# A mixture-of-experts stage whose gathered and scattered rows move as 1 KB quarters, with VectorE turning them and the down weights stationary

## The chip, the cores and the metric

The kernel runs on one core of one Trainium2 chip. The metric is the device time of one launch in microseconds (us). Only the last stage of the kernel, the mixture of experts, is touched by the change, along with the few instructions that lead into it.

## The reference

One layer of a hybrid decoder: an input projection, a depthwise convolution branch and an RWKV-7 recurrence branch, an output projection and a LayerNorm give `x` for 520 tokens (512 prompt tokens and 8 sample tokens) of width 1024, all in float32. Then the part that matters here:

```
scores = sigmoid(x @ router_w)                 # 64 experts, top 8 per token by groups
gates  = chosen scores / their sum * 2.5
for each expert e, for the tokens t that chose it:
    h = silu(x[t] @ exp_gate[e]) * (x[t] @ exp_up[e])        # 1024 -> 256
    f[t] += gates[t, e] * (h @ exp_down[e])                  # 256 -> 1024
f += shared expert;   y = LayerNorm(ALPHA * x + f)
```

There are 520 x 8 = 4160 pairs of token and expert, 65 per expert in the mean.

## The kernel before

**Stages.** Up to some 475 us the core projects, convolves, runs the recurrence, mixes, routes and computes the shared expert. `x` is written to DRAM as `scr_x1`, the residual with the shared expert as `scr_f`. Then the expert stage runs 64 jobs, one per expert, each with up to `CAP` = 96 tokens (an overflow path for experts with more tokens follows it; its loops are skipped at run time when there are none). The last stage reads `scr_f` back, normalises it and stores the result.

**One job q.** Its steps, each in a function of its own:

- `build_member` (VectorE) compares each token's position in the expert's list with 0 to 95 and so makes a 0/1 matrix of tokens by slots. `make_list` (TensorE) multiplies it with a table, so that each of the 96 slots gets its token's tile, row and weight (the weight in three bfloat16 parts). `read_list` (VectorE) turns that into a row number (slots without a token get a number past the end, which the DMA skips) and a weight.
- `gather` (GpSimd) fetches the 96 rows of `scr_x1`, 4 KB each, with one indirect DMA, into `x_list`: slots on partitions, 1024 columns along. `turn_list` (TensorE, eight transposes into PSUM) and `copy_turned` (ScalarE, two copies) make `x_list_t`: columns on partitions, slots along.
- `gate_up` (TensorE): weights stationary, in halves of 64 columns that land on partitions 0 to 63 and 64 to 127, the 96 slots moving; 128 instructions. `gate_act` (ScalarE sigmoid) and `gate_mul` (VectorE, two products) make `hid`.
- `down` (TensorE): `hid` stationary, 96 columns, the down weights moving, 512 at a time, 8 instructions. The result has slots on partitions. `weigh_act` (ScalarE) and `weigh_dve` (VectorE) multiply one half each by the gates on the way out of PSUM, into `y_list`, which has two buffers.
- `add_rows` (GpSimd) adds the 96 rows to `scr_f` with one accumulating indirect DMA. It waits for the scatter of the job before, as two experts may add to one row of `scr_f`, and an accumulating DMA reads before it writes.

**What sets the order.** Each engine has one queue with the jobs written out in order. For TensorE, at each q: the list of job q+4, gate_up of q+1, the turn of q+2, down of q. For GpSimd: the gather of q+4, then the scatter of q. For VectorE: read_list of q+4, gate_mul of q+1, build_member of q+5, weigh_dve of q. SyncE loads the weights, 1 MB each for gate, up and down, into six slots: gate and up of job q+6 are issued when gate_up(q) is done, down of q+5 when down(q-1) is done. `gathered`, `added` and the others are semaphores; a DMA raises its own by 16 when it has landed.

**Lines in the profile.** L2303 is the matmul of gate_up, L2331 that of down, L2278 the transposes, L869 make_list, L882 to L890 read_list, L858 build_member, L2312 gate_act, L2319 and L2321 gate_mul, L2288 copy_turned, L2341 and L2349 the two weighs, L900 the gather, L2358 the scatter, L913, L919 and L925 the loads of gate, up and down.

## Time and profile before

| | |
|---|---|
| time, median of 3 runs | 1145.57 us (1140.51 to 1149.66) |
| profiled execution, its span | 1144.7 us (its time outside the span is not shown) |
| TensorE busy | 1076.1 us, 94% |
| VectorE, ScalarE, GpSimd busy | 540.9, 280.5, 180.2 us |
| moved by the DMA engines | 278.79 MB |
| packets of GpSimd's DMA queue (q0) | 14336, 34.11 MB |

The span runs from the first to the last instruction. GpSimd's busy time is that of issuing its DMAs, not of their transfers. "Landing" in the DMA views is the time from an issue until its semaphore has risen.

### The profile page before, as it was taken

What the parts mean: (1) busy time and instruction counts of PE and PEld (TensorE: products, weight loads), DVE (VectorE), ACT (ScalarE), POOL (GpSimd) and SP (SyncE); (2) the same over time, 40 slices, a digit from 0 to 9 for tenths busy, and PEclk for the clock granted to TensorE, in tenths of its full rate; (3) what the DMA queues carried; (4) which work ended last, traced back from release to release, by engine and by line L of the source; (5) the groups of instructions that cost most, each with busy time, mean ns of one, the idle gap of its engine ahead of it and who ended that gap; (6) DMA issues with size and microseconds to landing.
All of it is one profiled execution on the core that took longest, in us unless ns stands there. A gap on an engine that the chain in (4) does not pass through costs nothing.

```text
span 1144.7 us, 33418 instructions
## 1 busy us (share of the span) xinstructions
PE 1076.1 (94%) x14942; PEld 814.8 (71%) x14943; DVE 540.9 (47%) x1208; ACT 280.5 (25%) x596; POOL 180.2 (16%) x198
## 2 busy tenths in 40 slices
PE   7999998887899999999999999999999999999990
PEld 6877886765653567677777777777777777777760
DVE  0789969698665778553222222222222222222215
ACT  2156411122337111111111111111111111111114
POOL 2000100000000002122222222122222222222210
PEclk9999999989669999999999999999999999999995
DMA  7222131220425557799999999999999999999734
GB/s 215 74 56 56 50 82 41 49 74 5 162 74 203 172 191 299 282 351 372 368 355 357 362 363 362 359 361 359 366 361 368 364 362 360 363 363 352 221 48 160
DMA packets 87365, 278.79 MB, mean 244 GB/s; under 512 B 22331, under 2 KB 46916, under 8 KB 62381
## 3 DMA queue, kind: packets, MB, share of 16 engines
q1 hardware_dynamic: 71941, 239.29, 57.1%
q0 software_dynamic: 14336, 34.11, 12.6%
q10 hardware_dynamic: 944, 3.24, 0.8%
q8 instruction: 119, 1.95, 0.7%
q14 instruction: 25, 0.20, 0.1%
HBM read 258.80 MB, written 34.52 MB: 256 GB/s over the span
## 4 chain that ended last, share of the span: by engine, by line
PE 67%; DVE 9%; issue 2%; ACT 2%; DMA 1%; SPq 0%; POOLq 0%; DVEq 0%; ACTq 0%
PE ph L2303 30%; PE ph L2331 19%; PE pst L2278 4%; PE ph L1496 2%; PE pz_late L2278 2%; DVE w_exp L163 2%; PE pt L869 1%; PE pst L1392 1%; PE pt L1411 1%; PE ph L1621 1%; PE ph L1478 1%; PE pz_late L1436 1%; PE pz_late L1437 1%; PE pt L1405 1%; PE pt L1414 0%
## 5 line engine op out<-in xcount | busy, mean ns | idle before, releaser
L2303 PE MATMUL ph<-arena,w_exp 128*64 128x96 f32 x8192 | 352.5, 247 | 0.0
L2303 PEld LDWEIGHTS ph<-arena,w_exp 128*64 128x64 f32 x8192 | 340.4, 138 | 4.2 <-issue 3.1
L2331 PE MATMUL ph<-w_exp,arena 128*96 128x512 f32 x512 | 230.5, 593 | 1.2 <-DVE arena L2321 1.2
L2358 POOL DMA_INDIRECT scr_f<-arena,row x64 | 92.3, 1443 | 472.0 <-DMA scr_f<-arena,row 230.1
L2319 DVE TENSOR_TENSOR arena<-arena,ph 128x192 f32<-128x192 f32 x64 | 22.7, 355 | 287.8 <-ACT arena L2312 287.8
L507 PE MATMUL pz<-w_exp 128*128 128x260 f32 x672 | 158.4, 394 | 0.3 <-ACT w_exp L322 0.3
L2331 PEld LDWEIGHTS ph<-w_exp,arena 128*96 128x96 f32 x512 | 80.2, 167 | 103.8 <-issue 102.3
L507 PEld LDWEIGHTS pz<-w_exp 128*128 128x128 f32 x672 | 129.3, 195 | 23.3 <-issue 2.9
L2349 DVE TENSOR_SCALAR arena<-ph,weight 96x512 f32<-96x512 f32 x64 | 47.8, 746 | 174.2 <-PE ph L2331 174.1
L2312 ACT ACTIVATE arena<-ph 128x192 f32<-128x192 f32 x64 | 21.1, 330 | 416.0 <-PE ph L2303 416.0
L163 DVE SCALAR_TENSOR_TENSOR w_exp<-arena,w_exp 128x512 f32<-128x512 f32 x120 | 90.0, 750 | 3.8
L900 POOL DMA_INDIRECT x_area<-scr_x,row x64 | 62.8, 982 | 39.4 <-issue 33.9
L2341 ACT ACTIVATE arena<-ph,weight 96x512 f32<-96x512 f32 x64 | 43.6, 682 | 86.1 <-PE ph L2331 76.6
L1496 PE MATMUL ph<-w_exp 128*128 128x512 f32 x128 | 57.9, 605 | 0.0
L2278 PE MATMUL pst<-ident,x_area 96*128 96x96 f32 x320 | 50.8, 289 | 0.0
L869 PEld LDWEIGHTS pt<-table,member 128*96 128x96 bf16 x320 | 24.3, 124 | 36.1 <-issue 35.7
L2278 PEld LDWEIGHTS pst<-ident,x_area 96*128 96x128 f32 x320 | 40.3, 202 | 7.6 <-issue 0.4
L2288 ACT COPY arena<-pst 128x480 f32<-128x480 f32 x64 | 35.7, 558 | 39.5 <-PE pst L2278 39.5
L1496 PEld LDWEIGHTS ph<-w_exp 128*128 128x128 f32 x128 | 24.3, 195 | 29.6 <-issue 29.0
L858 DVE TENSOR_TENSOR member<-slot_index,position 128x480 bf16<-128x480 f32 x64 | 41.6, 651 | 0.0
L2278 PE MATMUL pz_late<-ident,x_area 96*128 96x96 f32 x192 | 31.8, 275 | 0.0
L1478 PE MATMUL ph<-x_area,w_exp 128*128 128x260 f32 x128 | 29.1, 385 | 0.7 <-ACT arena L1826 0.7
(359 smaller groups left out, 1076.4 us busy)
## 6 DMA issues: line engine op xcount, KB each, us to landing
w_exp<-in_exp_up_dram SPq DMA_DIRECT2D x64, 1024.0 KB, 17.3
w_exp<-in_exp_down_dram SPq DMA_DIRECT2D x64, 1024.0 KB, 16.5
w_exp<-in_exp_gate_dram SPq DMA_DIRECT2D x64, 1024.0 KB, 13.7
w_exp<-in_w_in_dram SPq DMA_DIRECT2D x22, 512.0 KB, 3.9
w_exp<-in_x_prompt_dram SPq DMA_DIRECT2D x8, 512.0 KB, 5.2
w_exp<-in_w_out_dram SPq DMA_DIRECT2D x2, 2048.0 KB, 11.5
scr_x<-arena SPq DMA_DIRECT2D x4, 512.0 KB
scr_f<-arena ACTq DMA_DIRECT2D x4, 512.0 KB, 3.6
```

What stands on the lines that cost most here:

```text
L163: self.ch.link(self.nc.vector.scalar_tensor_tensor(out, u, w, out, ALU.mult, ALU.add))
L507: last = nc.tensor.matmul(banks(pz[0:w, c % 2, :])[:, b, :], m.w_col[:, c % WB, k, 0:w], halves(m.x_t[:, k, :])[:, b, :], start=(k == 0), ...
L858: nc.vector.tensor_tensor(m.member[:, s % 2], m.slot_index[:].unsqueeze(1).broadcast_to([P, NT, CAP]), src.unsqueeze(2).broadcast_to([P, N ...
L900: nc.gpsimd.indirect_dma_start(m.x_list[:, s, :], None, m.scr_x1, bass.IndirectOffsetOnAxis(ap=m.row[:, job.l:job.l + 1], axis=0), bounds_ ...
L1478: last = nc.tensor.matmul(banks(ph[:, 1 - part, :])[:, b, :], sh_w[part][:, k, j * P:(j + 1) * P], halves(x1_t[:, k, :])[:, b, :], start=( ...
L1496: last = nc.tensor.matmul(ph[0:n, i % 2, c * 512:(c + 1) * 512], lhs, w_out[c][:, kw, :], start=(part == 0 and k == 0), stop=(part == 1 an ...
L2278: last = nc.tensor.transpose(px[bank][:, at * CAP:(at + 1) * CAP], v[:, k, :], m.ident[0:CAP, 0:CAP])
L2303: last = nc.tensor.matmul(pgu[64 * half:64 * half + 64, s % 2, (2 * part + j) * CAP:(2 * part + j + 1) * CAP], w[job.slot][:, k, f0:P * ha ...
L2331: last = nc.tensor.matmul(pyl[0:CAP, c, :], hid[:, s % 2, j, :], m.expert_down[job.slot][:, j, c * 512:(c + 1) * 512], start=(j == 0), sto ...
L2341: nc.scalar.activation(y_list[:, s % 2, 0:512], pyl[0:CAP, 0, :], ACT.Copy, scale=weight[:, job.l:job.l + 1]).then_inc(y_act, 1)
L2349: nc.vector.tensor_scalar(y_list[:, s % 2, 512:1024], pyl[0:CAP, 1, :], weight[:, job.l:job.l + 1], None, ALU.mult).then_inc(y_dve, 1)
L2358: nc.gpsimd.indirect_dma_start(m.scr_f, bass.IndirectOffsetOnAxis(ap=row[:, job.l:job.l + 1], axis=0), y_list[:, s % 2, :], None, bounds_c ...
```

## The change

- `x_list` becomes `x_pieces`: each gathered row of 4 KB is fetched as four quarters of 1 KB (`QUADS`, `QW` = 256). Partition 32 * quad + t of run r holds quarter `quad` of slot 32 * r + t, so one indirect DMA fetches 32 slots, 128 pieces, and a job has three (`RUNS`). The scatter does the same with three DMAs that all raise `added`; `add_rows` of the next job waits for all three.
- VectorE turns 32 x 32 blocks (`turn_pieces`) straight into `x_list_t`; the eight transposes and the two copies go.
- `down` holds the down weights stationary in 64-column halves and moves `hid` (96 columns): 64 instructions of gate_up's form, in two PSUM areas by turns (the banks of the old transposes serve as the second). The result has columns on partitions; `turn_y` (VectorE, two turns) turns it back into `y_pieces`, and `weigh` (ScalarE, three activations in place) multiplies by the gates.
- `make_list` holds the table stationary and moves the member matrix, so that the list comes out along the free dimension; `read_list` turns it with one 32 x 96 VectorE transpose and writes row numbers and weights four times, one for each quarter.
- The order on VectorE becomes: read_list of q+4, turn_pieces of q+2, build_member of q+5, gate_mul of q+1, turn_y of q. The counting of overflow jobs moves into the stage; some small tiles move into other memory.

The core of the diff:

```
+QUADS = 4
+QW = D // QUADS
+RUNS = CAP // 32
 def make_list(...):
-        last = nc.tensor.matmul(pl[0:CAP, s % 2, 0:6], m.member[:, s % 2, i, :],
-                                m.table[:, bass.ds(q, 1), i, :].rearrange("p o c -> p (o c)"),
+        at = (q * NT + i) * 6
+        last = nc.tensor.matmul(pl[0:32, s % 2, 0:CAP], m.table_rows[:, at:at + 32], m.member[:, s % 2, i, :],
                                 start=(i == 0), stop=(i == NT - 1))
 def read_list(...):
-    nc.vector.tensor_copy(entry[:, s, :], pl[0:CAP, s % 2, 0:6]).then_inc(m.entry_ready, 1)
+    nc.vector.transpose(entry[:].rearrange("t r j -> t (r j)"), pl[0:32, job.s % 2, 0:CAP]).then_inc(m.entry_ready, 1)
     dve.wait_ge(m.entry_ready, q + 1)
-    (tensor_scalar, scalar_tensor_tensor, tensor_tensor, tensor_reduce of 96 x 1)
+    ch.link(nc.vector.scalar_tensor_tensor(found[:, :, 0], entry[:, :, 0], float(P), entry[:, :, 1], ALU.mult, ALU.add))
+    ch.link(nc.vector.scalar_tensor_tensor(found[:, :, 0], entry[:, :, 2], -float(TT), found[:, :, 0], ALU.mult, ALU.add))
+    for quad in range(QUADS):
+        last = nc.vector.tensor_scalar(m.piece_row[32 * quad:32 * (quad + 1), s, :], found[:, :, 0],
+                                       float(QUADS), float(QUADS * TT + quad), ALU.mult, ALU.add)
+    last.then_inc(m.pieces_ready, 1)
+    ch.link(nc.vector.tensor_reduce(found[:, :, 1], entry[:, :, 3:6], AX, ALU.add))
+    for quad in range(QUADS):
+        last = nc.vector.tensor_copy(m.piece_weight[32 * quad:32 * (quad + 1), s, :], found[:, :, 1])
+    last.then_inc(m.weight_ready, 1)
 def gather(...):
-    nc.gpsimd.indirect_dma_start(m.x_list[:, s, :], None, m.scr_x1, ...).then_inc(m.gathered[s], 16)
+    for r in range(RUNS):
+        nc.gpsimd.indirect_dma_start(m.x_pieces[:, s, r, :], None, m.scr_x1.rearrange("t (q c) -> (t q) c", q=QUADS),
+                                     bass.IndirectOffsetOnAxis(ap=m.piece_row[:, job.l, r:r + 1], axis=0),
+                                     bounds_check=QUADS * TT - 1, oob_is_err=False).then_inc(m.gathered[s], 16)
-    def turn_list(pe, job): ...      def copy_turned(act, job): ...
+    def turn_pieces(dve, job):
+        q, s = job.q, job.s
+        dve.wait_ge(gathered[s], 16 * RUNS * (job.turn + 1))
+        if job.has_before(2):
+            dve.wait_ge(gu_done, q - 1)
+        nc.vector.transpose(x_list_t[:, s % 2].rearrange("p k (r t) -> p r k t", r=RUNS),
+                            m.x_pieces[:, s].rearrange("p r (c k) -> p r k c", k=KD)).then_inc(x_ready, 1)
 def down(pe, job):
+        if job.has_before(2):
+            pe.wait_ge(y_turned, 2 * (q - 1))
+        for k in range(KD):
+            bank, at = (0, k) if k < KA else (1, k - KA)
             for j in range(2):
-                last = nc.tensor.matmul(pyl[0:CAP, c, :], hid[:, s % 2, j, :], m.expert_down[job.slot][:, j, c * 512:(c + 1) * 512], ...)
+                for half in range(2):
+                    d0 = 512 * half + k
+                    last = nc.tensor.matmul(py_t[s % 2][bank][64 * half:64 * half + 64, at * CAP:(at + 1) * CAP],
+                                            m.expert_down[job.slot][:, j, d0:512 * half + 512:KD], hid[:, s % 2, j, :], ...)
-    def weigh_act(act, job): ...     def weigh_dve(dve, job): ...
+    def turn_y(dve, job):
+        for bank, (k0, k1) in enumerate(((0, KA), (KA, KD))):
+            dve.wait_ge(y_done, 2 * q + bank + 1)
+            if job.has_before(2) and bank == 0:
+                dve.wait_ge(added[s % 2], 16 * RUNS * job.pair)
+            nc.vector.transpose(y_pieces[:, s % 2].rearrange("p r (c k) -> p r k c", k=KD)[:, :, k0:k1, :],
+                                py_t[s % 2][bank][:, 0:(k1 - k0) * CAP].rearrange("p (k r t) -> p r k t", r=RUNS, t=32)).then_inc(y_turned, 1)
+    def weigh(act, job):
+        act.wait_ge(y_turned, 2 * q + 2)
+        act.wait_ge(weight_ready, q + 1)
+        for r in range(RUNS):
+            last = nc.scalar.activation(y_pieces[:, s % 2, r, :], y_pieces[:, s % 2, r, :], ACT.Copy,
+                                        scale=piece_weight[:, job.l, r:r + 1])
+        last.then_inc(y_weighed, 1)
 def add_rows(pool, job):
-        pool.wait_ge(y_act, q + 1)
-        pool.wait_ge(y_dve, q + 1)
+        pool.wait_ge(y_weighed, q + 1)
         if job.has_before(1):
-            pool.wait_ge(added[(s + 1) % 2], 16 * job.before)
+            pool.wait_ge(added[(s + 1) % 2], 16 * RUNS * job.before)
-        nc.gpsimd.indirect_dma_start(m.scr_f, ..., y_list[:, s % 2, :], ..., compute_op=ALU.add).then_inc(added[s % 2], 16)
+        for r in range(RUNS):
+            nc.gpsimd.indirect_dma_start(m.scr_f.rearrange("t (q c) -> (t q) c", q=QUADS),
+                                         bass.IndirectOffsetOnAxis(ap=piece_row[:, job.l, r:r + 1], axis=0), y_pieces[:, s % 2, r, :], None,
+                                         bounds_check=QUADS * TT - 1, oob_is_err=False, compute_op=ALU.add).then_inc(added[s % 2], 16)
```

## Rows read from the trace of the kernel before

**Rows 1.** The page: busy time and share of each engine, and DMA in 40 slices.

```profile
PE 1076.1 (94%) x14942; PEld 814.8 (71%) x14943; DVE 540.9 (47%) x1208; ACT 280.5 (25%) x596; POOL 180.2 (16%) x198
DMA  7222131220425557799999999999999999999734
```

**Rows 2.** Chain of waits, 700 to 712 us: start, length, what.

```profile
699.92 5.43 PE ph L2303 x128
705.36 0.72 PE pst L2278 x5
706.08 0.33 PE pz_late L2278 x3
706.42 3.44 PE ph L2331 x8
709.85 0.18 PE pt L869 x5
710.04 1.96 PE ph L2303 x43
```

**Rows 3.** Timeline of GpSimd, 700 to 760 us: start, length, what, idle before.

```profile
702.45 1.44 POOL L2358 DMA_INDIRECT scr_f<-arena,row  x1 [6.70 <-DMA scr_f<-arena,row]
704.19 0.98 POOL L900 DMA_INDIRECT x_area<-scr_x,row  x1 [0.30 <-issue]
713.12 1.44 POOL L2358 DMA_INDIRECT scr_f<-arena,row  x1 [7.95 <-DMA scr_f<-arena,row]
```

**Rows 4.** The scatter: landings in 490-560 us, 640-1040 us (with GpSimd's wait), 1118-1121 us.

```profile
DMA to landing us min/median/max: 6.8/7.7/9.0
...
  DMA scr_f<-arena,row: 227.0, 30
...
DMA to landing us min/median/max: 7.9/9.3/10.4
...
DMA to landing us min/median/max: 4.9/4.9/4.9
```

**Rows 5.** DMA queues, 700 to 760 us: packets, MB, share of 16 engines.

```profile
q1 hardware_dynamic: 2534, 18.45, 80.9%
q0 software_dynamic: 1309, 3.04, 20.6%
```

**Rows 6.** DMA queue 1, 20 to 60 us, packets of 512 bytes.

```profile
q1 hardware_dynamic: 5258, 2.65, 24.4%
```

**Rows 7.** Timeline of SyncE's queue, and the last down load's landing (1060 to 1072 us).

```profile
477.21 0.33 SPq L913 DMA_DIRECT2D w_exp<-in_exp_gate_dram  x1
...
1063.85 0.33 SPq L925 DMA_DIRECT2D w_exp<-in_exp_down_dram  x1
...
DMA to landing us min/median/max: 15.0/15.0/15.0
```

**Rows 8.** Timeline: first scatter, last weigh, last scatter, first load of the last stage.

```profile
489.28 1.50 POOL L2358 DMA_INDIRECT scr_f<-arena,row  x1 [8.37 <-DVE row L889]
...
1118.02 0.75 DVE L2349 TENSOR_SCALAR arena<-ph,weight 96x512 f32<-96x512 f32 x1 [3.77 <-PE ph L2331]
...
1119.61 1.40 POOL L2358 DMA_INDIRECT scr_f<-arena,row  x1 [6.27 <-DVE arena L2349]
1124.64 2.15 SPq L2389 DMA_DIRECT2D w_exp<-scr_f  x5
```

**Rows 9.** Stretches of 10 us: busy PE, PEld, DVE, ACT, POOL, clock, DMA share, GB/s.

```profile
240.00:250.00 10.00, 8.23 (x175) 6.04 (x172) 9.55 (x15) 2.69 (x4) 0.00 (x0) 0.68 0.05 13
700.00:710.00 10.00, 10.00 (x151) 7.70 (x149) 2.54 (x10) 1.87 (x4) 2.41 (x2) 1.00 1.03 360
```

**Rows 10.** Groups of instructions, 700 to 760 us: busy us, mean ns | idle before.

```profile
L2349 DVE TENSOR_SCALAR arena<-ph,weight 96x512 f32<-96x512 f32 x6 | 4.5, 746 | 16.9 <-PE ph L2331 16.9
L2341 ACT ACTIVATE arena<-ph,weight 96x512 f32<-96x512 f32 x6 | 4.1, 682 | 7.2 <-PE ph L2331 7.2
...
L885 DVE TENSOR_SCALAR spare<-entry,minus_spare,spare_row 96x1 f32<-96x1 f32 x6 | 1.6, 269 | 0.2
L889 DVE TENSOR_TENSOR row<-spare,token 96x1 uint32<-96x1 f32 x6 | 0.9, 155 | 0.2
```

More of the change, by code:

```diff
@@ L833, in lists @@
     m.x_area = sb("x_area", [P, KD * TT])
-    m.x_list = m.x_area[0:CAP, 0:NB * D].rearrange("t (s d) -> t s d", s=NB)
+    m.x_pieces = view(m.x_area, 0, NB, RUNS, QW)
+    m.AT_BEHIND = NB * RUNS * QW
+    m.job_expert = view(m.x_area, m.AT_BEHIND, m.EXTRA)
     m.member = sb("member", [P, 2, NT, CAP], BF16)
-    m.entry = sb("entry", [CAP, STEPS, 6])
-    m.row = sb("row", [CAP, STEPS], U32)
-    m.spare = sb("spare", [CAP, STEPS])
-    m.token = sb("token", [CAP, STEPS])
-    m.weight = sb("weight", [CAP, STEPS])
+    m.entry = sb("entry", [32, RUNS, 32])
+    m.found = sb("found", [32, RUNS, 2])
+    m.piece_row = sb("piece_row", [P, STEPS, RUNS], U32)
+    m.piece_weight = sb("piece_weight", [P, STEPS, RUNS])
     m.member_ready = sem("member_ready")
@@ L877, in read_list @@
     q, s = job.q, job.l
-    entry, spare, token, row, weight = m.entry, m.spare, m.token, m.row, m.weight
+    entry, found = m.entry, m.found
     dve.wait_ge(m.list_done, q + 1)
     if job.has_before(STEPS):
-        dve.wait_ge(m.added[s % 2], 16 * (job.pair - STEPS // 2 + 1))
-    nc.vector.tensor_copy(entry[:, s, :], pl[0:CAP, s % 2, 0:6]).then_inc(m.entry_ready, 1)
+        dve.wait_ge(m.added[s % 2], 16 * RUNS * (job.pair - STEPS // 2 + 1))
+    nc.vector.transpose(entry[:].rearrange("t r j -> t (r j)"), pl[0:32, job.s % 2, 0:CAP]).then_inc(m.entry_ready, 1)
@@ L1835, in store_f @@
                     act.dma_start(m.scr_f[t0:t0 + n, :], x1[0:n, i, :]).then_inc(m.f_stored[i], 16)
-                for i in range(TM - 1):
+                for i in range(TM):
                     store_f(i)
-                work.copy_turned(act, Job(0))
-                store_f(TM - 1)
                 act.wait_ge(f_done, NT)
@@ L1844, in _ @@
                 last.then_inc(sample_moved, 1)
-                work.copy_turned(act, Job(1))
                 store_f(TM)
@@ L2165, in experts @@
     hid = view(m.arena, m.AT_INVERSE + 4 * CAP, 2, 2, CAP)
-    y_list = view(m.arena, m.AT_X1, 2, D)[0:CAP]
+    y_pieces = view(m.arena, m.AT_X1, 2, RUNS, QW)
     jobs3 = view(m.arena, m.AT_X1 + 2 * D, m.EXTRA, E)
@@ L2185, in experts @@
     o_gate, o_up, o_down = m.expert_gate[0], m.expert_up[0], m.expert_down[0]
-    o_place = sb("o_place", [P, NT])
-    o_entry = sb("o_entry", [CAP, 6])
+    o_at = m.AT_BEHIND + m.EXTRA
+    o_place = view(m.x_area, o_at, NT)
+    o_entry = view(m.x_area, o_at + 8, 6)[0:CAP]
     o_row = sb("o_row", [CAP, 1], U32)
-    o_spare = sb("o_spare", [CAP, 1])
-    o_token = sb("o_token", [CAP, 1])
-    o_weight = sb("o_weight", [CAP, 1])
-    o_x_list = x_list[:, 0, :]
+    o_spare, o_token, o_weight = (view(m.x_area, o_at + 16 + i, 1)[0:CAP] for i in range(3))
+    assert o_at + 19 <= KD * TT
+    o_x_list = m.x_area[0:CAP, 0:D]
     o_x_list_t = x_list_t[:, 0]
@@ L2195, in experts @@
     o_hid = hid[:, 0]
-    o_y_list = y_list[:, 0, :]
+    o_y_list = view(m.arena, m.AT_X1, D)[0:CAP]
     o_member = m.member[:, 0]
@@ L2326, in down @@
         pe.wait_ge(m.down_loaded[job.slot], job.filled)
-        for c in range(2):
-            if job.has_before(1):
-                pe.wait_ge((y_act, y_dve)[c], q)
+        if job.has_before(2):
+            pe.wait_ge(y_turned, 2 * (q - 1))
+        for k in range(KD):
+            bank, at = (0, k) if k < KA else (1, k - KA)
             for j in range(2):
-                last = nc.tensor.matmul(pyl[0:CAP, c, :], hid[:, s % 2, j, :], m.expert_down[job.slot][:, j, c * 512:(c + 1) * 512],
-                                        start=(j == 0), stop=(j == 1))
-            last.then_inc(y_done, 1)
@@ L2475, in vector @@
                 count_jobs(q)
-            weigh_dve(dve, Job(q))
+            turn_y(dve, Job(q))
             if q + 2 == E:
@@ L2535, in scalar @@
                 gate_act(act, Job(q + 1))
[L2536 to L2537 removed]
+            weigh(act, Job(q))
             if q + 2 == E:
@@ L2705, in kernel_program @@
         m.cnt = sb("cnt", [P, 4, E])
-        m.table = sb("table", [P, E, NT, 6], BF16)
+        m.table_rows = sb("table", [P, E * NT * 6 + 32], BF16)
+        m.table = view(m.table_rows, 0, E, NT, 6)
         m.w_exp = sb("w_exp", [P, SLOTS * EXPERT_FLOATS])
```

112 lines of the change are left out of this document (37 added, 75 removed).

## Prediction

> **What bounds the kernel now.** I read the views from coarse to fine. The page's busy line and slices come first [rows 1]: TensorE is busy 94% of the span, GpSimd 16%, and from the middle of the span on the DMA row stands at 9 in every slice. In a 10 us window of the stage TensorE is busy all 10.00 us at full clock and the DMA share is 1.03 [rows 9]. So in the expert stage TensorE and the DMA engines are both full, and it must be settled which of them a shorter TensorE job would leave as the limit. The reader should see there that "TensorE 94%" is not yet an answer.
>
> The chain of waits gives TensorE's job [rows 2]. From one gate_up to the next (699.92 to 710.04) is 10.12 us: 5.43 for 128 gate and up matmuls, 1.05 for eight transposes (0.72 and 0.33), 3.44 for the eight down matmuls, 0.18 for the list. Nothing waits in between. Sixty-four such jobs are the stage.
>
> GpSimd's timeline [rows 3] shows the second chain, which the share of 16% hides. add_rows(q) may be issued only when the scatter of q-1 has landed, so scatters are serial: issued at 702.45 for 1.44 us, the next at 713.12, a period of 10.67. The tile view has the landing [rows 4], and it counts from the start of the issue: the last scatter starts at 1119.61, lands 4.9 later, and the loads of f that wait for it start at 1124.64 [rows 8]. Taken from the end of the issue, a landing is 7.7 - 1.4 = 6.3 us early in the stage (median), 9.3 - 1.4 = 7.9 in the middle and 3.5 for the very last, which has the DMA engines to itself. Between a release and the issue GpSimd loses another 0.9: weigh_dve ends at 1118.02 + 0.75 = 1118.77, the scatter starts at 1119.61 [rows 8]. So the middle stands at 1.4 + 7.9 + 0.9 = 10.2 us per job and more in single ones. In that stretch GpSimd waited for a scatter 30 times, 227.0 us [rows 4]. This chain is already as long as TensorE's job; the spare buffer of y_list lets it lag a little.
>
> The DMA view gives the third [rows 5]. In 60 us, 5.93 jobs of 10.12, the weight queue took 80.9% and GpSimd's queue 20.6% of 16 engines: together 1.015 x 60 / 5.93 = 10.3 us of DMA per job. The loads tell the same another way [rows 7]: job 6's gate is issued at 477.21, the last down weights at 1063.85, and they land 15.0 later, at 1078.9: 602 us for 58 jobs, 10.38 each. They never had slack to go faster. Three resources thus sit between 10.1 and 10.7 us per job, and the change shortens one of them.
>
> **The change part by part.** TensorE: the eight transposes go (-1.05). The down product becomes 64 instructions (8 k x 2 j x 2 halves, two instructions each as in gate_up) of the very form of gate_up, 64 columns stationary, 96 moving: 64 x 5.43/128 = 2.71, against 3.44 (-0.73). The list's five matmuls move 96 columns in place of 6: bounded by 0.18 as now and by 5 x 0.042 x 2 = 0.42; I take 0.3. TensorE's job is 5.43 + 2.71 + 0.3 = 8.4 us, 1.7 less. If TensorE alone were the limit, that would be 64 x 1.7 = 109 us. It is not.
>
> VectorE: in a 10 us window it is busy 2.54 [rows 9]. Out go weigh_dve (0.75) and the old read_list (five instructions, 0.15 to 0.27, about 0.87) [rows 10]. In come the new read_list, twelve instructions of 0.15 to 0.27 (1.8 to 3.2), and two turns of 768 elements per partition each, for which no row exists: at the 746 ns of 512 elements [rows 10] each is 1.1, and twice that is my upper end for the strided read and write. Sum: 0.92 + 1.8..3.2 + 2.2..4.4 = 4.9 to 8.5 us. I take 6.3. That fits beside the other work, and nothing behind it on the engine is late: gate_mul(q+1) is needed only after gate_up(q+2). If the turns cost three times my row, it would stand at 10 and join the others.
>
> ScalarE: the two copies and one weigh go, three weighs of 256 elements come, each at most the 0.68 of the 512-element one [rows 10]: with what stays, at most some 2.4 us of a job, free either way. Dropping the job counting ahead of the first residual gives VectorE about 3 us back and the longer read_lists take about that; I count 0. The arena moves, table padding and the overflow path cost nothing here: no overflow job runs in the trace.
>
> GpSimd: each gather and each scatter becomes three indirect DMAs of 128 rows of 1 KB in place of one of 96 rows of 4 KB. The issue of 96 rows takes 1.44 (scatter) and 0.98 (gather) [rows 3]. For 128 rows the cost lies between the same and 128/96 of it: 1.44 to 1.92, and 0.98 to 1.31. With 0.3 between neighbours (704.19 against the end of the scatter before it), a job's scatters take 4.9 to 6.4 us to issue and the gathers 3.8 to 4.8. I take 5.6 and 4.3, since a list of row addresses is written out entry by entry and half of the step is the middle. GpSimd would be busy near 9 us of a job, not 2.4.
>
> DMA work: the bytes stay. The descriptors do not: now 1309 packets of GpSimd's queue in 5.93 jobs are about 221, by the layout 192 rows and 32 completions. After, 6 x 128 rows and 96 completions make 864, 640 more. What one more costs beside its bytes is at least nothing, and at most what a whole 512-byte packet takes, 24.4% x 16 x 40 us / 5258 = 29.7 ns [rows 6]: 640 / 16 x 0.0297 = 1.2 us per job. I take 0.6, so 10.9 us of DMA per job.
>
> The serial scatter chain is then what ends last. Its period is the issue of all three pieces, the landing of the third from the end of its issue, and GpSimd's 0.9: add_rows waits for all 48 completions of a job, not 16. The landing is bounded by 3.5, the quiet end, and 7.9, the loaded middle [rows 4, 8]. The last piece carries a third of the bytes, but its two forerunners are queued before it and the weight queue shares the engines. With the period above the DMA work per job, the weight queue is empty part of the time, which is nearer to the early stretch (6.3) and the quiet end than to the middle: I take 5.6. Period 5.6 + 5.6 + 0.9 = 12.1 us; ends 4.9 + 3.5 + 0.9 = 9.3 (then another resource decides) and 6.4 + 7.9 + 0.9 = 15.2. The gathers' 4.3 us of issue hide inside the 5.6 of landing. What waits behind: turn_y(q) on VectorE waits for the scatter of q-2, and down(q+2) for turn_y(q), so the whole stage falls into step, TensorE idling 4 us of each job.
>
> The sum, on the profiled execution (span 1144.7, 0.9 below the median of the three runs; the rest of the difference I leave out). First scatter at 489.3 [rows 8]; 63 periods of 12.1 = 762.3; the last issue 5.6 and a quiet landing 3.5; and from there to the end of the span what it takes now, 1144.7 - (1119.6 + 4.9) = 20.2. Together 1280.9, say 1280 us, +135.
>
> One rule of the Trainium skill speaks the other way on the landing. By the page "DMA: Bandwidth & Descriptors", section "Anatomy of one DMA", a GpSimd-issued DMA takes about 2.0 us plus its bytes at 436 GB/s: an estimate of 2.3 us for one 128 KB piece, and a period of 8.8, which would be no limit at all. For the present 384 KB it gives 2.9; the quiet landing of 3.5 comes near that, the loaded 7.9 is nearly three times as long, so the trace agrees only where nothing else moves, and I keep the rows. The same page, "Rules for kernel authors", asks to coalesce small transfers into large ones; the change does the reverse.
>
> **The rivals.** (a) The pieces land quickly, the chain hides, and DMA work decides. The condition is a chain under about 10.9, which the low ends allow (9.3). The loads would then end at 1078.9 + 58 x (0 to 1.2), and after them come the last down (2.7), turn (1.1), weigh (1.3), GpSimd's 0.9, issue (5.6), landing (3.5) and the 20.2: 1078.9 + 35.3 = 1114.2, up to 1184; with 0.6 it is 1149. For it: the last piece is small, and the load queue is deep now only because it is saturated. Against: a saturated queue is just what lengthens landings, 6.3 to 7.9 in the same kernel.
>
> (b) The faster side of that, under 1134: it holds only if a quarter row costs nearly nothing beside its bytes (less than 0.34 us a job) and the chain stays under 10.4. Then the gain is at most 31 us, since the loads can't end before 1079: TensorE's 109 us can't be had in any case. I see no row for both conditions at once.
>
> (c) The small pieces get one turn each beside 8 KB weight packets. A job has 48 such turns per engine and the weight queue only 24 packets, so pieces lag, landing grows past 7.9 and the period is 14.5 to 16: 489.3 + 63 x 15 + 29.3 = 1464. In its favour, the 7.9 of now is already long for six rows per engine. A second mechanism leads to the same place: with TensorE idle a third of the time its granted clock may fall to half, as it did in a window ahead of the stage, 0.68 with 8.23 us busy of 10 [rows 9]; 8.4 us of work at a mean of 0.6 is 14.
>
> (d) VectorE's turns cost three times my row and more (over 3.3 us each) and VectorE at 11 us or above becomes the limit: like the forecast in time, and told from it by a VectorE that is busy over 90%.
>
> **How the numbers follow.** A chain period of 11.1 to 13.9 (1218 to 1394), the forecast, with (d) in it: 0.62. (a) without its fast part, 1134 to 1184, and the stretch up to 1218: 0.18. (b): 0.08. (c): 0.12. The range leaves out (b), the part of (a) under 1145, and most of (c): 1145 to 1405. A measurement of this kernel can tell about 1% from no change, 11.5 us either way (its three runs span 0.8%): faster by more than that needs under 1134, 0.09; within it 1134 to 1157, 0.07; slower 0.84.
>
> **What would show it.** Right, if GpSimd's share rises from 16% to over 60%, its queue shows near 55,300 packets (864 x 64, from 14,336), three scatter issues of 1.4 to 1.9 us stand together, the next three some 12 us later, VectorE's turn_y waits for the scatter, TensorE's job shows 5.43 + 2.71 with a gap of about 4 us, and the DMA row falls below 9. Wrong in the landing if the period is about 11 with the DMA row at 9; wrong in the issue if the pieces take under 1 us or over 2; wrong altogether if TensorE stays without gaps at 8.4.

## Result, and the profile after

The changed kernel takes 1323.6 us (median of four runs, 1317.3 to 1326.0); the kernel before takes 1147.2 in the same comparison. The ratio is 1.153, with a 95% interval of 1.148 to 1.158. The forecast was 1280 us.

The page of the changed kernel, beside [rows 1] and [rows 5]: busy time by engine, clock and DMA by slice, and the two queues.

```profile
PE 1106.5 (84%) x18014; PEld 981.0 (75%) x18015; DVE 789.6 (60%) x1784; ACT 260.3 (20%) x596; POOL 531.2 (40%) x455
...
PEclk9989998887999989899889889889889889889985
DMA  6211222104646679889888898879789879888534
...
q1 hardware_dynamic: 71941, 239.29, 50.3%
q0 software_dynamic: 36864, 34.20, 13.8%
```

No engine is full any more. TensorE fell from 94 to 84% of the span, the DMA row is no longer all nines, and the clock row alternates 9 and 8. GpSimd's queue went from 14,336 to 36,864 packets.

One stretch of 300 us in the expert stage, before and then after (columns as in [rows 9]):

```profile
700.00:1000.00 300.00, 300.00 (x4459) 232.83 (x4458) 78.96 (x270) 55.21 (x119) 70.54 (x58) 1.00 1.02 363
```

```profile
700.00:1000.00 300.00, 249.22 (x4533) 243.17 (x4531) 150.65 (x414) 35.79 (x92) 181.19 (x138) 0.89 0.87 288
```

TensorE was busy without a gap at full clock; now it is busy 249 us at a mean granted clock of 0.89. The DMA share fell to 0.87, so the weight queue is no longer kept full.

The period comes from the first scatter issue of the first and of the last job. The timeline of the changed kernel, GpSimd and the first load of the last stage:

```profile
491.66 1.64 POOL L2353 DMA_INDIRECT scr_f<-arena,piece_row  x1 [9.86 <-ACT arena L2342]
...
1286.18 1.55 POOL L2353 DMA_INDIRECT scr_f<-arena,piece_row  x1 [2.75 <-issue]
...
1289.91 1.56 POOL L2353 DMA_INDIRECT scr_f<-arena,piece_row  x1 [0.30 <-issue]
1293.80 2.15 SPq L2385 DMA_DIRECT2D w_exp<-scr_f  x5
```

(1286.18 - 491.66) / 63 = 12.61 us per job. In the kernel before it was (1119.61 - 489.28) / 63 = 10.01 [rows 8]. 63 x 2.60 = 164 us of the 170.5 by which the span grew (1144.7 to 1315.2). "Period" below is always this quotient; it is a mean over the whole stage, and the jobs of the stretch from 700 to 1000 us are a little longer (23 of them here, 13.0 us each).

The same timeline from 804 us on shows what ends a period:

```profile
804.45 1.07 DVE L2334 STREAM_TRANSPOSE arena<-pst 128x480 f32<-128x480 f32 x1 [5.79 <-DMA scr_f<-arena,piece_row]
...
805.21 1.63 POOL L2353 DMA_INDIRECT scr_f<-arena,piece_row  x1 [3.30 <-issue]
...
807.14 1.57 POOL L2353 DMA_INDIRECT scr_f<-arena,piece_row  x1 [0.30 <-issue]
...
809.02 1.58 POOL L2353 DMA_INDIRECT scr_f<-arena,piece_row  x1 [0.30 <-issue]
...
810.84 0.39 PE L874 MATMUL pt<-member,table 128*32 128x96 bf16 x5 [2.00 <-DVE member L862]
...
818.23 1.59 DVE L2334 STREAM_TRANSPOSE arena<-ph 128x480 f32<-128x480 f32 x2 [6.80 <-DMA scr_f<-arena,piece_row]
...
818.99 1.62 POOL L2353 DMA_INDIRECT scr_f<-arena,piece_row  x1 [4.34 <-issue]
```

Three issues end at 810.60. The DMA lands, VectorE's turn_y starts at once (818.23, 7.6 later), and the next job's first issue follows 0.76 behind it. "issue" in GpSimd's row is its own latency after a wait that just ended; the release is seen on the VectorE row. TensorE's idle time has moved to the list: VectorE stands in turn_y's wait, so build_member behind it is late and the list waits for it. The waits of 700 to 1000 us sum this up (us, times, longest):

```profile
DVE arena L2334 <- DMA scr_f<-arena,piece_row: 142.1, 23, 9.2
...
PE pt L874 <- DVE member L862: 50.2, 16, 5.4
```

TensorE's work in one early job, at full clock (timeline):

```profile
484.31 0.39 PE L874 MATMUL pt<-member,table 128*32 128x96 bf16 x5
484.63 5.51 PE L2291 MATMUL ph<-arena,w_exp 128*64 128x96 f32 x128
489.96 2.60 PE L2322 MATMUL pst<-arena,w_exp 128*64 128x96 f32 x40
492.40 1.64 PE L2322 MATMUL pz_late<-arena,w_exp 128*64 128x96 f32 x24
493.97 0.39 PE L874 MATMUL pt<-member,table 128*32 128x96 bf16 x5
```

From start to start: 0.32 for the list, 5.33 for gate_up, 4.01 for down, 9.66 together. Groups of the stretch from 700 on, to be read beside [rows 2] and [rows 10]:

```profile
L2291 PE MATMUL ph<-arena,w_exp 128*64 128x96 f32 x2946 | 151.1, 272 | 0.2 <-issue 0.2
L2322 PE MATMUL ph<-arena,w_exp 128*64 128x96 f32 x768 | 49.3, 285 | 0.3 <-issue 0.3
...
L2276 DVE STREAM_TRANSPOSE arena<-x_area 128x768 f32<-128x768 f32 x23 | 36.2, 1572 | 0.8 <-DMA x_area<-scr_x,piece_row 0.2
```

gate_up's mean is 272 ns, against 247 in the kernels whose stretch has full clock. That is the lower clock: the list and gate_up that follow a wait of 3.46 us, from 824.50 on, run with the clock halved (the row below, 0.50), while the gate_up from 811.15 on, at 1.00, takes 5.50 us as a whole. The turn of x stands at 1.57 us.

```profile
824.00:829.00 5.00, 4.50 (x55) 4.36 (x57) 1.06 (x3) 0.00 (x0) 3.48 (x4) 0.50 0.92 270
```

### The profile page after: what moved, and what is told of

Same layout as the page of the kernel before. It is cut to its first block and busy times, and to the rows that moved or that the text cites. A ratio compares the mean times of both kernels' runs of the same rounds, so it can differ in the third digit from the quotient of the medians.

```text
span 1315.2 us, 40523 instructions
## 1 busy us (share of the span) xinstructions
PE 1106.5 (84%) x18014; PEld 981.0 (75%) x18015; DVE 789.6 (60%) x1784; ACT 260.3 (20%) x596; POOL 531.2 (40%) x455
## 3 DMA queue, kind: packets, MB, share of 16 engines
q0 software_dynamic: 36864, 34.20, 13.8%
## 5 line engine op out<-in xcount | busy, mean ns | idle before, releaser
L2291 PE MATMUL ph<-arena,w_exp 128*64 128x96 f32 x8192 | 409.6, 268 | 6.4 <-issue 6.4
L2353 POOL DMA_INDIRECT scr_f<-arena,piece_row x192 | 306.0, 1594 | 265.6 <-issue 247.1
L2291 PEld LDWEIGHTS ph<-arena,w_exp 128*64 128x64 f32 x8192 | 397.5, 155 | 13.1 <-issue 7.2
L908 POOL DMA_INDIRECT x_area<-scr_x,piece_row x192 | 200.1, 1042 | 73.0 <-issue 72.7
L2342 ACT ACTIVATE arena<-arena,piece_weight 128x256 f32<-128x256 f32 x192 | 83.7, 498 | 682.0 <-DVE arena L2334 682.0
L2334 DVE STREAM_TRANSPOSE arena<-pst 128x480 f32<-128x480 f32 x32 | 34.2, 1069 | 196.7 <-DMA scr_f<-arena,piece_row 187.7
L2322 PE MATMUL ph<-arena,w_exp 128*64 128x96 f32 x2048 | 131.3, 285 | 0.4 <-issue 0.3
L2322 PEld LDWEIGHTS ph<-arena,w_exp 128*64 128x64 f32 x2048 | 128.3, 219 | 0.6 <-issue 0.5
L2276 DVE STREAM_TRANSPOSE arena<-x_area 128x768 f32<-128x768 f32 x64 | 101.0, 1577 | 9.1 <-DMA x_area<-scr_x,piece_row 7.3
L2322 PE MATMUL pst<-arena,w_exp 128*64 128x96 f32 x1280 | 84.6, 288 | 4.5 <-DVE arena L2309 4.4
L2322 PEld LDWEIGHTS pst<-arena,w_exp 128*64 128x64 f32 x1280 | 81.5, 219 | 4.9 <-DVE arena L2309 4.6
L896 DVE COPY piece_weight<-found 32x3 f32<-32x3 f32 x256 | 56.9, 222 | 4.9
L2322 PE MATMUL pz_late<-arena,w_exp 128*64 128x96 f32 x768 | 53.0, 288 | 0.0
```

What stands on the lines that cost most here:

```text
L896: last = nc.vector.tensor_copy(m.piece_weight[32 * quad:32 * (quad + 1), s, :], found[:, :, 1])
L908: nc.gpsimd.indirect_dma_start(m.x_pieces[:, s, r, :], None, m.scr_x1.rearrange("t (q c) -> (t q) c", q=QUADS), bass.IndirectOffsetOnAxis( ...
L2276: nc.vector.transpose(x_list_t[:, s % 2].rearrange("p k (r t) -> p r k t", r=RUNS), m.x_pieces[:, s].rearrange("p r (c k) -> p r k c", k=K ...
L2291: last = nc.tensor.matmul(pgu[64 * half:64 * half + 64, s % 2, (2 * part + j) * CAP:(2 * part + j + 1) * CAP], w[job.slot][:, k, f0:P * ha ...
L2322: last = nc.tensor.matmul(py_t[s % 2][bank][64 * half:64 * half + 64, at * CAP:(at + 1) * CAP], m.expert_down[job.slot][:, j, d0:512 * hal ...
L2334: nc.vector.transpose(y_pieces[:, s % 2].rearrange("p r (c k) -> p r k c", k=KD)[:, :, k0:k1, :], py_t[s % 2][bank][:, 0:(k1 - k0) * CAP]. ...
```

## Experiments

Times are medians; the ratio with its interval is to the kernel before in the same comparison. Each kernel's row of 700 to 1000 us has the columns shown above.

**1. two_targets.** Even and odd jobs add into two tensors, so a scatter never waits for the one ahead of it. The odd experts' part is left out of the result.

```
-        if job.has_before(1):
-            pool.wait_ge(added[(s + 1) % 2], 16 * RUNS * job.before)
-            nc.gpsimd.indirect_dma_start(m.scr_f.rearrange(...
+            nc.gpsimd.indirect_dma_start((m.scr_f, m.scr_g)[s % 2].rearrange(...
```

> The changed kernel, with even experts added into scr_f and odd ones into a second tensor, both filled with the same residual; the last stage reads only the first, so the odd experts' part is left out of y. add_rows no longer waits for the scatter of the job before, only (through turn_y) for the one two jobs back. Serial scatter chain (my theory): the period of 12.6 us falls to the next limit, GpSimd's own six issues (about 9.7 us), TensorE's 9.65 us or the DMA work (10.4 to 10.9): 10.5 us, time near 1190. Rival, TensorE with its throttled clock is the limit: TensorE's job is untouched, time stays above 1290. Rival, DMA work is already the limit: also above 1290.

Measured: 1268.1 us, ratio 1.108 (1.104 to 1.112), period 11.69. The window:

```profile
700.00:1000.00 300.00, 272.61 (x4979) 252.47 (x4976) 169.10 (x465) 42.30 (x103) 199.02 (x151) 0.98 0.94 309
```

TensorE's timeline of the same kernel (start, length, what, idle before):

```profile
804.90 2.11 PE L2292 MATMUL ph<-arena,w_exp 128*64 128x96 f32 x45
807.27 0.33 PE L2292 MATMUL ph<-arena,w_exp 128*64 128x96 f32 x2 [0.26 <-issue]
808.02 0.39 PE L2292 MATMUL ph<-arena,w_exp 128*64 128x96 f32 x4 [0.43 <-issue]
808.76 0.41 PE L2292 MATMUL ph<-arena,w_exp 128*64 128x96 f32 x4 [0.35 <-issue]
```

The chain was a limit: without it 55 us go, and no wait for a scatter is left. But the time stays 78 us above what I expected, and neither rival (above 1290) holds. The new thing is in the rows: in the middle of gate_up TensorE pauses, about every 0.74 us, for 0.2 to 0.45 us, and the profile names nothing that it waits for. None of my cases had this.

**2. few_weight_bytes.** From the seventh job on only an eighth of each expert's weights is loaded (the rest of a slot keeps older weights); the chain stays.

```
+    n = KD * FE if q < SLOTS else KD * FE // 8
-    ...gate[s].rearrange("p k f -> p (k f)"), one_expert(m.exp_gate, q))
+    ...gate[s].rearrange("p k f -> p (k f)")[:, 0:n], one_expert(m.exp_gate, q)[:, 0:n])
```

> The changed kernel, with only an eighth of each expert's weights loaded from job 6 on (the rest of a slot keeps old weights, so y is another). Same instructions and waits, 7 MB in place of 58 x 3 MB. If the landing of a scatter is long because the weight packets share the engines, it falls from 7.6 to about 3.5 us after the last issue, the period to 5.4 + 3.5 + 0.8 = 9.7 us, and the time to about 1140. If a landing is long by itself (small descriptors, read and write of scr_f), the period stays near 12.6 and the time at 1310 to 1325.

Measured: 1268.6 us, ratio 1.109 (1.104 to 1.114), period 11.69.

```profile
700.00:1000.00 300.00, 273.00 (x4964) 253.85 (x4966) 167.18 (x451) 40.95 (x100) 199.49 (x151) 0.98 0.41 77
```

Its gate_up in the same stretch, from the groups:

```profile
L2294 PE MATMUL ph<-arena,w_exp 128*64 128x96 f32 x3239 | 165.6, 253 | 24.8 <-issue 24.5
```

The time is neither of the two that I expected (an eighth of 58 x 3 MB is 22 MB, not the 7 written there, which changes nothing in the argument). With the DMA engines at 0.41 the landings are short enough that the chain drops out. GpSimd's timeline:

```profile
813.48 1.55 POOL L2356 DMA_INDIRECT scr_f<-arena,piece_row  x1 [0.30 <-issue]
...
819.38 1.63 POOL L2356 DMA_INDIRECT scr_f<-arena,piece_row  x1 [0.30 <-issue]
```

The third piece is issued until 815.03, and the next job's first piece starts at 819.38, right behind three gathers, without having waited, so the landing took under 4.4 us. The same stretch, from the end of the last issue to the release, is 7.6 in the timeline above. So much of a landing is contention with the weight queue. The rest is the same as in experiment 1 to 1 us: the same period and the same pauses (24.5 against 24.4 us of the stretch). The second limit is not DMA load.

**3. down_contiguous.** The 64 stationary columns of down lie side by side, not 8 apart; y has its columns permuted.

```
-                    d0 = 512 * half + k
-                   m.expert_down[job.slot][:, j, d0:512 * half + 512:KD], ...
+                    d0 = 512 * half + 64 * k
+                   m.expert_down[job.slot][:, j, d0:d0 + 64], ...
```

> The changed kernel, with down's stationary operand read as 64 neighbouring columns instead of every eighth (the columns of y come out in another order). The profile shows down at 4.0 us where 2.7 was counted; if the stride is what makes it dear, down shows about 2.7 us here. Serial scatter chain: TensorE is not what ends last, so the time moves by less than 1% (1310 to 1330), unless the longer idle time lowers its clock further. Rival, TensorE is the limit: 64 x 1.3 = 83 us less, near 1240.

Measured: 1321.5 us, ratio 1.156 (1.150 to 1.161): no change from the changed kernel, as the chain theory has it. The groups of its TensorE:

```profile
L2322 PE MATMUL ph<-arena,w_exp 128*64 128x96 f32 x768 | 34.2, 246 | 0.4 <-issue 0.4
...
L2322 PEld LDWEIGHTS ph<-arena,w_exp 128*64 128x64 f32 x768 | 32.8, 137 | 0.6 <-issue 0.6
```

Those 768 matmuls took 49.3 us in the changed kernel and take 34.2 here; a weight load falls from 219 to 137 ns. gate_up, whose columns lie 2 apart, has 138 ns in the kernel before, whose whole stage runs at full clock. So a stride of 8 floats costs, and one of 2 doesn't.

**4 and 5. before_two_issues, before_four_issues.** The kernel before, with only its scatter cut into two issues of 512 columns or four of 256.

```
+        for r in range(n):
+            c = slice(1024 // n * r, 1024 // n * (r + 1))
+            ...indirect_dma_start(m.scr_f.rearrange("t (q c) -> (t q) c", q=n), ...part_row[:, job.l, r:r + 1]...,
+                                  y_list[:, s % 2, c], None, ...
```

> The kernel before, whole in every part but the scatter, which goes out as two indirect DMAs of 96 half rows of 2 KB (VectorE makes the two index columns). Serial scatter chain: issue 2 x 1.44 + 0.3 = 3.2 us, landing 6.3 to 7.9, 0.9 for GpSimd: period 10.4 to 12.0, time 1170 to 1270, near 1215. Rival, the cost of the change lies in the small descriptors, the turns or TensorE: at most 0.3 us of DMA work more per job, time 1145 to 1165.

> The kernel before, whole, with each job's scatter in four indirect DMAs of 96 quarter rows of 1 KB: as many descriptors as the changed kernel's scatter, one issue more. Theory: issue 4 x 1.41 + 0.9 = 6.5 us, landing after the last at least 4 and at most 7.5, GpSimd 0.8: period 11.3 to 14.8, time 1225 to 1440, near 1280. Two issues gave 10.35 per job; if a landing shrinks by as much as the issue grows, as it nearly did there, the period is 10.7 to 11 and the time 1185 to 1205.

Measured: 1166.2 us, ratio 1.019 (1.015 to 1.024), period 10.35, and 1298.4 us, ratio 1.133 (1.129 to 1.137), period 12.48. The four-issue kernel's window:

```profile
700.00:1000.00 300.00, 264.83 (x3582) 194.89 (x3581) 72.50 (x337) 43.65 (x96) 164.73 (x122) 0.93 0.92 296
```

Its longest waits:

```profile
ACT arena L2348 <- DMA scr_f<-arena,part_row: 174.3, 24, 12.0
DVE arena L2356 <- DMA scr_f<-arena,part_row: 164.5, 20, 11.3
```

And its gate_up:

```profile
L2310 PE MATMUL ph<-arena,w_exp 128*64 128x96 f32 x3072 | 132.1, 247 | 0.0
```

This is the chain theory by itself: one issue, two, four give 10.0, 10.35, 12.5 us per job. With one or two there is still slack (TensorE busy 298.4 of 300 with two), with four the chain is the limit. Two issues came out just below the range that I expected (1170 to 1270), since the slack swallowed most; four came out inside theirs. From two issues to four a job's issuing grows from 3.14 to 6.58 us, but what lies between its end and the next job's first issue shrinks from 7.27 to 5.80 (medians over the GpSimd timelines), so two more issues lengthen the period by 2.1 us, not by 3.4. Part of the 7.27 was slack, and early pieces can land while later ones are issued; how much is which is not shown. And a split scatter puts no pauses into gate_up (0.0).

**6 and 7. quarter_gather_only, quarter_gather_two_targets.** The changed kernel's gather in three pieces and VectorE's turn of x, with the down product, the weighing and the one whole-row scatter of before; in the second, two targets as well (odd experts left out).

```
-        for r in range(RUNS):
-            ...indirect_dma_start(m.scr_f.rearrange(...), ...piece_row[:, job.l, r:r + 1]..., y_pieces[:, s % 2, r, :], ...
+        ...indirect_dma_start(m.scr_f, ...row[:, job.l:job.l + 1]..., y_list[:, s % 2, :], ...
```

> The changed kernel with its second half undone: gather in 1 KB quarters and the VectorE turn stay, down, the two weighs and the scatter (one DMA of 96 rows of 4 KB) are those of the kernel before; both lists are made, which adds five small matmuls and five small VectorE instructions. Theory (the cost is the serial chain of a job's scatters): the chain is again 1.44 + 7.9 + 0.9 = 10.2 us, TensorE's job 9.4, DMA work 10.4: time 1140 to 1165. Rival (the small gather pieces lie in the queue ahead of the scatters and lengthen landings): period near 10.9, time near 1195. Rival (TensorE throttled or starved): above 1200.

> The kernel of quarter_gather_only, with odd experts added into a second tensor and no wait on the scatter before; the second tensor is left out of y. TensorE's job is 9.4 us, GpSimd about 6, the scatter chain spans two jobs. Theory: DMA work (10.4 us a job, loads end at 1079 or later) is what is left: 1110 to 1135, faster than before. Rival: the landings never mattered with whole rows, TensorE's 9.4 with gaps in its instruction supply leaves 1140 to 1160.

Measured: 1190.2 us, ratio 1.040 (1.035 to 1.044), period 10.59; and 1199.7 us, ratio 1.047 (1.044 to 1.049), period 10.72. Both missed my expectation. The first came near the 1195 of the rival by which small gather pieces lengthen the landings, but that cause doesn't hold, as the second shows. gate_up in the first, and the second's window:

```profile
L2301 PE MATMUL ph<-arena,w_exp 128*64 128x96 f32 x3560 | 169.4, 248 | 14.4 <-issue 13.6
```

```profile
700.00:1000.00 300.00, 284.24 (x4047) 202.66 (x4043) 146.69 (x471) 27.28 (x54) 125.53 (x111) 1.00 0.95 336
```

and its gate_up:

```profile
L2302 PE MATMUL ph<-arena,w_exp 128*64 128x96 f32 x3561 | 172.1, 248 | 14.6 <-issue 14.2
```

In the first GpSimd still waits for scatters; the second has no such wait and is no faster. The chain isn't its limit, the DMA share is 0.95, and gate_up pauses again. Set side by side over 640 to 1060 us, the timelines of TensorE and GpSimd show where the pauses lie. In experiments 1, 3, 6 and 7 gate_up has 286 pauses of 0.15 to 0.7 us, and every one begins between 0.9 us before and 4.5 us after the start of a job's third gather issue, 207 of them 0 to 3 us after it and 60 before it. Operations of VectorE lay over few of them in experiment 3 (5 of 43).

**8. before_two_targets.** The kernel before with two scatter targets (odd experts left out), a control.

> The kernel before with odd experts added into a second tensor and no wait on the scatter before; the second tensor is left out of y. TensorE's 10.11 us job stays and is the limit: 1130 to 1150, less than 1.5% from before. It is the control for the run before it.

Measured: 1142.9 us, ratio 0.998 (0.995 to 1.000), period 10.0, as expected:

```profile
700.00:1000.00 300.00, 300.00 (x4394) 230.91 (x4392) 79.54 (x270) 56.05 (x120) 70.36 (x59) 1.00 1.03 360
```

**9. before_four_gathers.** Is it the gather's split? The kernel before, with its gather alone cut into four issues of 256 columns.

```
+    for r in range(4):
+        nc.gpsimd.indirect_dma_start(m.x_list[:, s, 256 * r:256 * (r + 1)], None, m.scr_x1.rearrange("t (q c) -> (t q) c", q=4),
+                                     bass.IndirectOffsetOnAxis(ap=m.part_row[:, job.l, r:r + 1], axis=0), ...
```

> The kernel before, with only its gather cut into four issues of 256 columns; its scatter stays one issue, TensorE still turns x, and the result is the same. Theory: gate_up's pauses of 0.3 to 0.45 us, which every run with three gather issues shows within 3 us of the last of them, belong to the gather's issues. Then they appear here too, one to three in a job, and the period goes from 10.0 to 10.4 to 10.8 us: 1165 to 1190 us. Rival: they belong to what else those kernels share (VectorE's 1.57 us turn of x, its twelve small list operations, the list with 32 stationary columns). Then gate_up shows no pause, GpSimd's 5.9 us of issues a job hide beside TensorE, and the time is that of before within 1% (1140 to 1155 us).

Measured: 1247.0 us, ratio 1.093 (1.088 to 1.097), period 11.33. The window:

```profile
700.00:1000.00 300.00, 280.11 (x3868) 208.26 (x3866) 78.58 (x364) 44.10 (x104) 139.15 (x130) 1.00 0.90 318
```

GpSimd's group of gathers:

```profile
L910 POOL DMA_INDIRECT x_area<-scr_x,part_row x104 | 101.2, 973 | 32.3 <-issue 32.3
```

TensorE's timeline:

```profile
799.11 0.32 PE L2313 MATMUL ph<-arena,w_exp 128*64 128x96 f32 x3 [0.24 <-issue]
799.68 0.63 PE L2313 MATMUL ph<-arena,w_exp 128*64 128x96 f32 x8 [0.25 <-issue]
800.57 0.24 PE L2313 MATMUL ph<-arena,w_exp 128*64 128x96 f32 x1 [0.27 <-issue]
```

The pauses appear in a kernel whose TensorE, VectorE turn and scatter are those of before. GpSimd is busy under half of the time, and TensorE hardly ever waits for a gather (1.6 us in the whole stage). The direction is as the theory said, the size is larger: 1.3 us per job, not 0.4 to 0.8, and in this execution another 16 us ahead of the first scatter (505.40 against 489.28), which no run explains.

The DMA view of the same kernel, 798 to 799 us, lists one queue, that of the weights:

```profile
q1 hardware_dynamic: 55, 0.39, 109.0%
```

Yet gate_up's first pause of that job begins at 798.87. Of the 54 pauses of 0.15 to 0.7 us that TensorE makes in 640 to 1060 us, 26 have no packet of GpSimd's queue in flight, and in experiment 6 none of 62 overlaps a packet of 1036, 2056 or 3076 bytes, sizes that only its gathers have. The pauses go with the issues, and many fall where no gathered piece moves.

**10. two_targets_contiguous.** Experiments 1 and 3 together.

> The changed kernel with both the two scatter targets and the contiguous 64 stationary columns in down (y with its columns permuted, and the odd experts' part left out of the result). Theory: without the scatter chain TensorE is the limit, so the 1.2 us a job that the contiguous read takes from down (4.2 to 3.0 us) come off in full: 1268 - 63 x 1.2 = 1193 us, 1180 to 1210. Rival: the limit is how fast TensorE is given its instructions, or GpSimd's issues (9.7 us a job with three scatters and three gathers); then down's shorter time is given back in pauses and the time stays above 1245 us.

Measured: 1221.0 us, ratio 1.069 (1.065 to 1.072), period 10.97: between the two. 0.72 us per job come off, not 1.2:

```profile
L2292 PE MATMUL ph<-arena,w_exp 128*64 128x96 f32 x3430 | 183.2, 257 | 29.6 <-issue 28.6
```

TensorE decides once the chain is gone, but part of what down gives back is lost to more pauses (28.6 against 24.4 us of the stretch in gate_up, and 4.0 in down).

**11. two_targets_one_gather.** Experiment 1 with, from the fifth job on, only the first of the three gather issues; the other pieces of x are old rows.

```
-    for r in range(RUNS):
+    for r in range(RUNS if q < NB else 1):
```

> The changed kernel with two scatter targets, and from the fifth job on only the first of the three gather issues (the pieces of the other two keep old rows, so two thirds of x are stale, and the odd experts' part is left out of the result). TensorE's, VectorE's and ScalarE's instructions are the same as in the run with two targets. Theory: the pauses in gate_up come with the run of gather issues, so they go, and the period falls from 11.7 to between 10.0 and 10.7 us: 1165 to 1205 us. Rival: they come with TensorE's long run of small instructions (list, gate_up and 64-column down, some 197 pairs a job) whatever GpSimd does: the pauses stay and the time is above 1245 us.

Measured: 1126.9 us, ratio 0.986 (0.982 to 0.990), period 9.59: far under what the theory said, and under the kernel before.

```profile
700.00:1000.00 300.00, 299.67 (x6099) 293.90 (x6097) 199.56 (x559) 50.78 (x124) 181.01 (x124) 1.00 1.04 362
```

Its gate_up:

```profile
L2292 PE MATMUL ph<-arena,w_exp 128*64 128x96 f32 x3968 | 171.7, 247 | 0.3 <-issue 0.3
```

Same instructions on TensorE, VectorE and ScalarE, the same three scatters, and TensorE is busy 299.7 of 300 us without a pause. Its period is now its own work, the 9.66 of the early job. The two further gather issues cost 2.1 us per job and 141 us in all, 132 of them in the 63 periods. The run takes away issues and bytes together, so it doesn't say which of the two it is.

**12. before_empty_gathers.** Experiment 9 with, from the fifth job on, the indices of issues two to four past the last row, so that they move nothing; three quarters of x are old rows.

```
-   m.total[:, s:s + 1], 4.0, float(r), ALU.mult, ALU.add)
+   m.total[:, s:s + 1], 4.0, float(r + (0 if q < NB or r == 0 else 4 * TT)), ALU.mult, ALU.add)
```

> The kernel before with its gather in four issues, as in the run with four gathers (1247 us), but from the fifth job on the indices of issues two to four lie past the last row, so that these three move nothing: GpSimd executes the same number of issues, and three quarters of the gathered bytes and landed packets are gone (three quarters of x are old rows in those jobs). Theory: TensorE's pauses come with GpSimd's work of issuing gathers back to back. Then they stay, and the time is 1225 to 1250 us. Rival: they come with the landing of the gather's 1 KB packets. Then they go or shrink to a quarter, and the time is 1140 to 1170 us.

Measured: 1155.3 us, ratio 1.007 (1.003 to 1.010), period 10.0.

```profile
700.00:1000.00 300.00, 300.00 (x4401) 231.10 (x4402) 91.47 (x420) 55.87 (x119) 157.76 (x148) 1.00 0.99 345
```

Its gathers on GpSimd:

```profile
L910 POOL DMA_INDIRECT x_area<-scr_x,part_row x118 | 114.4, 970 | 36.6 <-issue 36.6
```

The theory named in the expectation falls. GpSimd spends the same 970 ns on each of four issues, 0.3 us apart, and TensorE has no pause. Nor is it the number of packets: GpSimd's queue has 19,456 in experiment 9 and here, with 34.15 and 22.19 MB. It takes further gather issues that have something to move. All bytes in one issue [rows 3], or a quarter of them in four, don't disturb TensorE; all bytes in three or four issues do.

## Why the prediction was right, and what it didn't see

The direction, the mechanism and the range held; 1280 was 3.3% low. By its steps:

- **The scatter chain ends last.** Shown: experiment 1 takes it away and 55 us go, experiments 4 and 5 bring it by themselves to a kernel without it. Its period was forecast at 5.6 + 5.6 + 0.9 = 12.1 and is 12.61. Three issues take 5.39 in the mean and from their end to the next job's first issue there are 7.22 (medians 5.37 and 7.58), of which some 0.8 lie between the release and the issue: the landing is 6.4 in the mean and 6.8 in the median job, not 5.6. The mis-sized term is this landing. I argued that the weight queue would be empty part of the time; it has a share of 65.5% in the stretch against 81.3% before, and that isn't empty enough.
- **The sum.** First scatter 491.7 (489.3 forecast), 63 periods 794.5 (762.3), last issues 5.3 (5.6), landing 2.3 (3.5), the rest 21.4 (20.2). The 63 periods carry the miss.
- **TensorE's job 8.4 us.** Wrong: 9.66. gate_up and the list (0.33) came as forecast; down takes 4.0 to 4.07, not 2.71, because I took gate_up's duration for a form that differed in its stride. So TensorE was relieved of 0.45 us, not 1.7. Behind the chain this didn't show (experiment 3). The gap, forecast at 4 us a job, is 2.2 in the stretch (50.8 us over 23 jobs), since the lower clock stretches the work as well.
- **VectorE 6.3 us.** 150.65 us for the 23 jobs of the stretch is 6.5. The turn of x takes 1.57 and the turn of y 1.07 + 0.69, together 3.3, in the middle of the 2.2 to 4.4 that I allowed, though both are above the 1.1 of my row. Rival (d) didn't occur.
- **GpSimd.** 1.59 us for a scatter of 128 rows, 1.04 for a gather, near the low end of both. It is busy 181.19 / 23 = 7.9 us of a job and 40% of the span, not 9 us and over 60%.
- **DMA work 10.9 us.** 0.87 x 300 / 23 = 11.3. But by another way: 36,864 packets, not 55,300, since up to four neighbouring pieces of a gather travel as one packet (packets of 2056, 3076 and 4096 bytes in the trace), while scattered pieces stay at 1024.
- **Rival (a)**, that with a short chain DMA work decides at 1114 to 1184, did not occur, as its condition, a period under about 10.9, wasn't met. Its price is refuted by experiments 1 and 2: without the chain the time is 1268, at a DMA share of 0.94 or of 0.41 alike. The floor of 1114 that I gave (b) wasn't undercut: experiment 11, with two thirds of the gathered bytes gone in most jobs, took 1127.
- **Rival (c)**, small pieces lagging behind 8 KB packets and a falling clock: in part. The landing, 6.8, stayed under the 7.9 of before, where (c) has it grow past that. The granted clock did fall, to 0.89 in the stretch, a mean of times at 2.4 and at 1.2 GHz, with TensorE idle ahead of the list in most jobs. It is 0.98 in experiment 1 and 1.00 in experiment 11, where these waits are gone. That it follows the gaps is my reading; no run changed it by itself.

**What no case of mine had:** a second cost, by these runs larger than the first (1268 to 1127 us in experiment 11, where taking the chain away gave 1324 to 1268). Three gather issues a job slow gate_up by pauses that nothing in the profile explains. In the changed kernel itself they are hidden (0.2 us of the stretch, where TensorE idles 50 us at the list anyway), so the comparison of before and after alone can't show them. Had only the chain been mended, the time would have stopped at 1268. Three gather pieces with a whole scatter cost 4.0% (experiment 6), a scatter in four issues 13.3% (experiment 5), the change with three of each 15.3%; these kernels differ in more than that, so whether the two costs add is not shown.

**What stays open** is how the gathered pieces hold TensorE. Shown is that it needs several gather issues that move data (experiments 9, 11, 12), and not DMA load (2), GpSimd's time (12), VectorE's turn or a down product in 64-column halves (9), or split scatters (5). Nor do the pieces have to be moving during a pause (the timing under 6 and 9). Whether the pauses are late instructions or a late read of TensorE's operands, I didn't separate; no packet of the profile's instruction queues is in flight during the pauses from 798.87 to 800.57 in experiment 9. Gathers spaced apart, and one issue for all three pieces, were not run. No version here that does the whole computation is faster than the kernel before, and experiment 8's 0.998 can't be told from it.

## What to carry to other kernels

Where read-modify-write scatters must follow one another, count issues and landing as one serial chain, however idle GpSimd looks. An extra issue adds 1.7 to 1.9 us of issuing per job (its own time and 0.30); from two issues to four (experiments 4 and 5) only about 1.1 us of it per issue reached the period, as slack and a shorter wait for the landing took up the rest. Splitting an indirect gather is not free either, even where GpSimd, the DMA engines and the consumer have slack; look at the busiest engine for short pauses put down to "issue". Take an instruction's price from a row with the same stride, not only the same shape.

## What the hardware showed unexpectedly

- TensorE's pauses: 0.2 to 0.45 us, about every 0.74 us, in runs of up to seven, around and behind the last of several gather issues, and in part while no gathered piece moves; 24.4 us in 300 (experiment 1), 0.3 with one issue (experiment 11), 0.0 with empty ones (experiment 12).
- An indirect gather whose indices are all out of bounds takes GpSimd as long to issue as a full one (970 against 973 ns).
- Issue time hardly grows with rows: 96 to 128 rows is 1.44 to 1.59 us for a scatter, 0.98 to 1.04 for a gather, and a quarter of the width saves almost nothing (medians 1.44 and 1.41 for 96 rows, experiment 5).
- The stationary operand's stride: 219 ns for a load with 32 bytes between elements, 137 for contiguous ones, 138 with 8 bytes. The Trainium skill, page "SBUF — State Buffer", section "Door 1: The DMA port swizzle", says that SBUF has 16-byte lines and that two accesses in the same line are needed for full speed; by that rule strides of 4 and 8 bytes are free and 32 is not, and these three rows agree.
- The Trainium skill, page "DMA: Bandwidth & Descriptors", section "Rules for kernel authors", advises to coalesce small transfers. Experiments 5 and 9 agree and give it a price in this kernel: 13.3% and 9.3% of the time for four issues in place of one.
